# Eight sums of u blocks in each feed-forward network made by GpSimd instead of the vector engine

## The reference

```python
def rms_norm(x, gain):
    xf = x.astype(jnp.float32)
    y = xf * lax.rsqrt(jnp.mean(xf * xf, axis=-1, keepdims=True) + EPS)
    return (y * gain.astype(jnp.float32)).astype(x.dtype)

def swiglu_ffn(u, w_gu, w_down):
    g, up = jnp.split(u @ w_gu, 2, axis=-1)
    return (jax.nn.silu(g) * up) @ w_down
...
        h = h + 0.5 * swiglu_ffn(rms_norm(h, ffn1_norm[l]), ffn1_w_gu[l], ffn1_w_down[l])
        h = h + token_mixing(...)
        h = h + 0.5 * swiglu_ffn(rms_norm(h, ffn2_norm[l]), ffn2_w_gu[l], ffn2_w_down[l])
```

## Time and profile before

| | us |
|---|---|
| median of 3 executions | 2697.83 (2688.76 to 2706.49) |
| the profiled execution | 2704.2 |
| its span | 2702.2 |
| network one, token mixing, network two | 0 to 755, 755 to 1988, 1988 to the end |

### The profile page before, as it was taken

The page is one execution under the profiler, slowest core; times in us unless marked ns, Lnnn a source line. Parts: engine busy times, 40 slices in busy tenths (PEclk is TensorE's granted clock), DMA queues, the critical chain, the costliest instruction groups (busy, mean ns, idle before and its releaser), DMA issues. The chain is left out here.

```text
span 2702.2 us, 37098 instructions
## 1 busy us (share of the span) xinstructions
PE 2456.1 (91%) x14204; PEld 2170.7 (80%) x14204; DVE 1420.8 (53%) x1993; ACT 938.9 (35%) x1557; POOL 556.2 (21%) x647
## 2 busy tenths in 40 slices
PE   5999999699969998988998989998969999995999
PEld 5999999699958887966777768886857888884887
DVE  6665566455455557433767652112167666663553
ACT  4333333233344444432434441112134333332331
POOL 0021121100023334221444453221201221221000
PEclk7999999799979999987999989999989999997999
DMA  4334444565330000010000011111223444437653
GB/s 168 122 140 159 153 144 147 203 247 187 123 118 9 25 25 0 1 32 10 4 7 4 4 40 55 47 47 39 87 101 121 149 163 160 155 132 263 216 195 117
DMA packets 124340, 278.05 MB, mean 103 GB/s; under 512 B 9424, under 2 KB 56400, under 8 KB 120864
## 3 DMA queue, kind: packets, MB, share of 16 engines
q1 hardware_dynamic: 124192, 276.03, 29.6%
HBM read 195.00 MB, written 80.86 MB: 102 GB/s over the span
## 5 line engine op out<-in xcount | busy, mean ns | idle before, releaser
L897 DVE TENSOR_TENSOR f_w_lo<-f_rw,f_w_hi 128x1024 fp32r<-128x1024 f32 x154 | 194.8, 1265 | 250.0 <-ACT f_w_hi L575 250.0
L737 PE MATMUL f_ps<-u_hi,f_w_hi 128*128 128x260 f32 (+1 forms) x1056 | 283.9, 323 | 19.3 <-DVE u_lo L834 15.3
L737 PE MATMUL f_ps<-u_lo,f_w_hi 128*128 128x260 f32 (+1 forms) x1056 | 282.6, 322 | 0.0
L737 PE MATMUL f_ps<-u_hi,f_w_lo 128*128 128x260 f32 (+1 forms) x1056 | 282.4, 322 | 0.0
L737 PE MATMUL f_ps<-f_far_hi,f_w_hi 128*128 128x260 f32 (+1 forms) x792 | 213.7, 324 | 24.3 <-DVE f_ev L910 13.5
L575 ACT CAST f_w_hi<-f_rw 128x1024 fp32r<-128x1024 f32 x154 | 161.2, 1047 | 153.9 <-PE f_ps L737 131.3
L737 PE MATMUL f_ps<-f_far_lo,f_w_hi 128*128 128x260 f32 (+1 forms) x792 | 212.6, 323 | 0.0
L737 PE MATMUL f_ps<-f_far_hi,f_w_lo 128*128 128x260 f32 (+1 forms) x792 | 212.4, 323 | 0.0
L737 PEld LDWEIGHTS f_ps<-u_hi,f_w_hi 128*128 128x128 f32 x1056 | 177.9, 192 | 38.7 <-issue 20.7
L737 PEld LDWEIGHTS f_ps<-u_lo,f_w_hi 128*128 128x128 f32 x1056 | 177.4, 191 | 14.1
L737 PEld LDWEIGHTS f_ps<-u_hi,f_w_lo 128*128 128x128 f32 x1056 | 177.1, 191 | 13.8
(11 more groups left out here) (370 smaller groups left out, 6300.8 us busy)
## 6 DMA issues: line engine op xcount, KB each, us to landing
f_rw<-in_gu SPq DMA_DIRECT2D x88, 512.0 KB, 4.5
f_rw<-kept_dsum SPq DMA_DIRECT2D x32, 704.0 KB, 5.0
f_rw<-kept_hid SPq DMA_DIRECT2D x35, 520.0 KB, 5.5
f_rw<-kept_hid SPq DMA_DIRECT2D x35, 512.0 KB, 5.5
f_rw<-in_down SPq DMA_DIRECT2D x24, 704.0 KB, 4.1
gt_raw<-in_gate SPq DMA_DIRECT2D x24, 512.0 KB, 3.5
h_in<-in_wd SPq DMA_DIRECT2D x11, 1024.0 KB, 5.3
kept_dsum<-h_in SPq DMA_DIRECT2D x44, 256.0 KB, 4.2
```

Source lines behind the costliest of these rows:

```text
L737: last = nc.tensor.matmul(out[:, b, 0:N], w[:, c], u[:, b * N:(b + 1) * N], start=(j in (0, 1, 5) and k == 0 and i == 0), stop=(k == 3 and ...
L897: nc.vector.tensor_tensor(slot(w_lo, st), src, slot(w_hi, st).bitcast(F32), ALU.subtract).then_inc(wlo_done, 1)
```

## The change

The eight sums (`mix_first` to `mix_fourth`, two instructions each) move from the DVE's program to the head of GpSimd's program, in both networks, with the same waits on the same semaphores and the same operands. DVE's program keeps the rest of its order.

```diff
         @block.gpsimd
         def _(pool):
+            def mix_first(q):
+                pool.wait_ge(u_done, 4 + 2 * q + 2)
+                pool.wait_ge(blo_done, q + 1)
+                nc.gpsimd.tensor_tensor(quarter(0, 0, q), quarter(0, 1, q), quarter(0, 0, q),
+                                        ALU.subtract).then_inc(mixed, 1)
+
+            def mix_second(q):
+                pool.wait_ge(u_done, 8 + 2 * q + 2)
+                pool.wait_ge(blo_done, 2 + q + 1)
+                pool.wait_ge(mixed, 2)
+                nc.gpsimd.tensor_tensor(quarter(0, 0, q), quarter(1, 1, q), quarter(0, 0, q),
+                                        ALU.subtract).then_inc(mixed, 1)
+
+            def mix_third(q):
+                pool.wait_ge(u_done, 8 + 2 * q + 2)
+                pool.wait_ge(mixed, 2)
+                nc.gpsimd.tensor_tensor(quarter(0, 1, q), quarter(1, 1, q), quarter(0, 1, q),
+                                        ALU.subtract).then_inc(mixed, 1)
+
+            def mix_fourth(q):
+                pool.wait_ge(u_done, 12 + 2 * q + 2)
+                pool.wait_ge(blo_done, 4 + q + 1)
+                pool.wait_ge(mixed, 4)
+                nc.gpsimd.tensor_tensor(quarter(0, 0, q), quarter(1, 0, q), quarter(0, 0, q),
+                                        ALU.subtract).then_inc(mixed, 1)
+
+            for mix in (mix_first, mix_second, mix_third, mix_fourth):
+                mix(0)
+                mix(1)
             for i in range(FP):
...
@@ -994,17 +997,11 @@
             u_lo(0, 1)
             weight_mix(1)
             scaled(0, 1)
-            mix_first(0)
-            mix_first(1)
             weight_lo(1)
             scaled(1, 1)
             u_lo(1, 0)
             u_lo(1, 1)
-            mix_second(0)
-            mix_second(1)
             weight_mix(2)
-            mix_third(0)
-            mix_third(1)
             u_lo(2, 0)
             u_lo(2, 1)
             weight_lo(2)
@@ -1018,8 +1015,6 @@
             scaled(1, 0)
             u_lo(5, 0)
             u_lo(5, 1)
-            mix_fourth(0)
-            mix_fourth(1)
             weight_lo(4)
```

More of the change, by code:

```diff
@@ L835, in u_lo @@
                                         u_pair(near_hi, far_hi, j, q).bitcast(F32), ALU.subtract).then_inc(blo_done, 1)
[L837 to L861, removed]
             def weight_mix(st):
```

## The result

Before, the median of 15 executions is 2701.28 us (2688.76 to 2716.84), and with the change 2712.05 us (2706.36 to 2721.28). The ratio is 1.0044, with a 95% interval of 1.0026 to 1.0063: 12 us slower, 7 to 17. That is within 1%, and inside the range. The sign and the mechanism are as predicted. The size is smaller than the +17 of the sum, which lies at the edge of the interval. The ratios leave out executions in a slower state, which comes with any kernel: here two, both in the experiments, 2740.10 us of the kernel before and 7086.19 us of the changed one, at mean granted clocks of 0.87 and 0.35.

The account below looks back on a forecast made before the run. Bound: the DVE's gapless program up to `f_w_lo` of step 4, then TensorE. Held instructions outweigh freed sums: +8.5 us per network, +17 on 2697.8, gives 2715 us, 0.6% slower; range 2700 to 2730 us.

Parts of the forecast that it names:

- the +17 of the sum: Whole kernel: +8.5 us delay of step 4 in each of two networks, together +17, giving 2715 us.
- (a): Up to the first `u_lo` of step 1: first pair leaves DVE, two scalings held 2.2 us each, net +2.1 us.
- my choice that the scaling is held too: DVE's three-operand scaling, both tensors in SBUF, is blocked by a POOL sum, adding 2.2 us per blocked instruction.
- rival 2: DVE scaling not held by POOL: +3.8 us for each network, 2705 us; chance 0.10.
- (b): Second and third pair: four POOL sums take turns with DVE; `f_w_lo` of step 2 ends 6.5 us late, at 67.9.
- (c): `f_w_lo` of step 2 to step 4: fourth pair leaves DVE, scaling and `u_lo` held; 18.6 us instead of 16.5.
- Rival 3: A two-row sum costs POOL more: at 3.4 us each, +16.6 us per network, 2731 us; chance 0.10.
- Rival 1: POOL sums overlap DVE freely: -6.6 us per network, 2685 us, faster by 0.5%; chance 0.07.
- Rival 4: The program's first POOL sum starts 6 us late in network one: +5.5 us on top, 2720 us; chance 0.05.
- the delay of `f_w_lo` of step 4 is the change of the whole time: Behind step 4 TensorE sets the pace, so this delay, +8.5 us per network, passes on in full.
- nothing is given back or added: Behind step 4: POOL's first weight sum starts over 20 us after the last new sum, so no further change.

Follow-up runs that it names:

- the fills: Changed kernel with each GpSimd sum replaced by three constant fills that read nothing, against the kernel before: 2691.35 us against 2703.83, ratio 0.9955.
- tiny sums: Changed kernel with each GpSimd sum cut to 8 of its 520 columns, against the kernel before: 2680.84 us against 2705.27, ratio 0.9911.

## Why the prediction was right, and where its size was off

**(a) The first pair.** Predicted +2.1, with the fourth scaling and the first of the next quarter held, and step 1 at 53.2. It starts at 53.05, the scalings take 4.94 and 4.88, and alone the pair gives +1.99. Right, and my choice that the scaling is held too was right: rival 2 falls.

**(b) The middle four.** Predicted ends of 56.6, 60.0, 63.4 and 66.8; they are 57.46, 53.04+6.82 = 59.86, 63.19 and 59.81+6.71 = 66.52. `f_w_lo` of step 2 was to end at 67.9 and ends at 67.61; alone the two pairs give +4.37 (4.4). The size is right. One turn was not as predicted: the first sum was to have the memory behind the second `u_lo`, ahead of the weight sum, and the weight sum went first. It is luck that this cost nothing: one weight sum and two POOL sums last as long in either order, and ScalarE's last wait there is for the second sum, 59.86 for 60.0.

**(c) The fourth pair.** Predicted +2.1, step 4 at 86.4 to 86.5. Alone +2.04; step 4 starts at 86.17. The sum of the three is +8.3 and +8.2, for +8.5 predicted (its parts, 2.1+4.4+2.1, make 8.6).

**Rival 3** (a sum costs POOL more). The second sum can only begin when `f_w_lo` of step 1 is done (45.74+1.21 = 46.95) and ends at 45.89+3.29 = 49.18: 2.23 us, not 3.4. It falls. **Rival 1** (free overlap) is what the fills show, and is not what sums do. **Rival 4** (6 us before the program's first POOL work): the first sum began at 42.38, 0.1 us after the second scaling, and held the fourth scaling at once. It isn't there. The Trainium skill (GPSIMD Engine Reference, Instruction dispatch) gives its 6 us for the first call of a freshly loaded kernel. Whether this sum is such a call no run shows; its trace has no such delay. A late start does exist in small (about 2 us, for the first of the middle sums and in some runs for the fourth pair), but not at this place.

**The step that was mis-sized** is the last one, "the delay of `f_w_lo` of step 4 is the change of the whole time". Of 16.5 us of delay 14.2 reached the first copies. Before's copies out of the accumulators are, in the timeline of ScalarE,

```profile
101.38 0.59 ACT L588 COPY h_in<-f_ps 128x520 f32<-128x520 f32 x1 [1.85 <-PE f_ps L737]
...
2063.40 0.59 ACT L588 COPY h_out<-f_ps 128x512 f32<-128x512 f32 x1 [1.97 <-PE f_ps L737]
```

and after:

```profile
108.82 0.59 ACT L617 COPY h_in<-f_ps 128x520 f32<-128x520 f32 x1 [1.84 <-PE f_ps L766]
...
2078.53 0.59 ACT L617 COPY h_out<-f_ps 128x512 f32<-128x512 f32 x1 [2.06 <-PE f_ps L766]
```

TensorE's clock behind step 4 accounts for it. Before, in network one and two (us, PE busy, granted clock, DMA share, GB/s):

```profile
77.30:84.00 6.70, 5.63 (x26) 0.50 0.23 77
2039.90:2046.70 6.80, 5.57 (x13) 0.50 0.23 64
```

and after:

```profile
84.20:91.00 6.80, 4.83 (x22) 0.50 0.07 12
2057.10:2060.40 3.30, 3.16 (x8) 0.50 0.00 0
```

Behind each of these the clock is at 1.00. Counted from the end of `f_w_lo` of step 4, the slow stretch lasted 6.2 and 6.1 us before, and 4.9 and 3.3 us after. At half the speed 2.8 us less of it are 1.4 us of work gained, which is the -1.45 of the table; in network one 1.3 us less are 0.7 of the -0.86. The same holds over seven profiles (before, the change twice, the first pair, the fourth pair, the added tiny instructions and the 14 added `u_lo`): the stretch from `f_w_lo` of step 4 to the first copy, less half of its slow time, is 20.2 to 20.6 us in network one and 19.6 to 19.8 in network two, while the slow time itself goes from 3.3 to 6.5 us. With the middle pairs alone it is 21.6 and 20.1 us, more than that; there TensorE stood still for another 0.4 us in network one before the copy. The prediction has no term for the clock behind step 4 ("nothing is given back or added"), and the waits there do hardly change (5.20 and 5.44 us).

The same error stands in two smaller numbers. I let step 1 last 8.5 us as before; it lasted 60.75-53.05 = 7.7, since the clock was at 0.62 in its first 5 us, where it had been 0.50. So the wait before step 2 is 6.92 and not 6.2. And steps 2 and 3 were to lose 2.5 us to the clock and lost 1.3 (67.67 to 80.73 is 13.06 us, against 11.8), so the wait before step 4 is 5.44 and not 4.3. Both are hidden by the waits and changed nothing in the sum, as the prediction said of the second.

The rest, from 14.2 us of the profiles to the 12 of the ratio, is inside its interval of 7 to 17 us. In network one the clock was slow for as long as before; it only fell sooner, 2.0 us ahead of the product of step 4 (84.2 and 86.17) where it had been 1.1 us (77.3 and 78.37), so more of it lay in the wait. In network two it was slow half as long. Why, these runs don't tell, and the length of the wait doesn't: behind the same 5.20 us in network one the slow stretch lasted 6.2 us in the kernel before and 3.4 with the first pair alone, and 6.4 behind the 21.71 us that the 14 added instructions made.

## What to carry to other kernels

Before work is moved to GpSimd to relieve the vector engine, look at where both read: if both read SBUF, each GpSimd instruction that meets a busy DVE takes a DVE slot of its own length, here 2.2 us lost for 1.15 us freed. In these traces "POOL is idle" was worth something only where the DVE was idle too, read PSUM, or where the GpSimd instruction read nothing. Another order brought the DVE's path nearly as much here as leaving the sums out: 0.993 with the same instructions on the same engines, against 0.991.

And measure such a change on the event that it moves (`f_w_lo` of step 4, good to 0.1 us), not on the whole time, which scatters by 13 to 16 us to either side of its median (2688.76 to 2716.84 before).

## What was not expected of the hardware

A sum on GpSimd that stands as begun can be passed by one or two DVE instructions and have the memory about 2 us late: the first of the middle sums wherever they ran on GpSimd, by one, and the first of the fourth pair by two where it came after 13 to 14 us without work (tiny sums) or 68 to 70 us (fourth pair alone, in both orders), but not after 10.5 us. Added 8-column instructions took that away, and the first pair, after 40 to 42 us, never had it, so idle time alone doesn't decide. GpSimd's fills of 128x1040 take 0.97 us and leave the DVE alone, while an 8-column subtraction still takes 0.58 us. The slow stretch of TensorE's clock behind waits of 5.1 to 5.6 us lasted between 3.3 and 6.5 us.
